# The sample state update of a gated linear recurrence mixer as two 32-row tiles of the array

## The chip, the core and the metric

One core of a Trainium2 chip runs the whole program. The metric is the device time of one execution in microseconds (us); the kernel before was timed three times.

## What is computed

The program is one inference step of a two-layer decoder: a recurrent mixer (HGRN2) and a convolutional feed-forward in layer 0, attention and feed-forward in layer 1, for a prompt of 512 tokens and for 8 sampled sequences of 8 tokens each. All of it is float32. The change lies in the mixer, in the state of the sampled sequences. For each of 8 heads (128 key and 128 value features) the reference does, cut to what matters:

```python
b = jnp.cumsum(lc, axis=2)                      # running log decay inside a chunk
o = (einsum('bhts,bhsv->bhtv', A, vc)           # inside the chunk
     + einsum('bhtd,bhdv->bhtv', qc * exp(b), S))
S = (exp(b_last)[..., None] * S                 # the old state, decayed
     + einsum('bhsd,bhsv->bhdv', kc * exp(b_last - b), vc))
o = rmsnorm(o, g_onorm) * silu(g)
```

For the sampled tokens there are 8 states of 128x128, one per sequence, and each sequence adds the product of its own 8 keys and 8 values. So with the 64 tokens of the samples side by side, token s may only reach the state of sequence s // 8.

## The kernel before

Five engines run programs written out by hand: SP issues the loads of weights, ACT and DVE work elementwise, POOL (GpSimd) too and issues some DMAs, PE multiplies. Semaphores order them; each engine takes its own work strictly in the order written. Tiles live in fixed places, PSUM is `acc` (four banks for the projections) and `aux` (four banks for all else, `aux[:, 0]` to `aux[:, 3]`).

The mixer is a pipeline over heads. `mixer(t, par, front, rec, tail)`, which every engine has, does in one block: `front`, the four projections of head t; `rec`, the recurrence of head t - 1 (masked products `gram` at seven levels, transposes of V and K, the prompt's state `ds`); `tail`, the end of head t - 2 (output products `outs`, the state update of the samples, the norm `onorm`). The blocks are mixer(1), a loop over mixer(2) to mixer(7), mixer(8) without projections, and mixer(9), which has only the tail. So mixer(2) to mixer(9) carry a tail each.

On PE a projection is `gemm` (L1353): for each of 8 slices of the inner dimension three pairs of products of 128x288 (the operands are split in a high and a low part), and the table `quarters` says after which slice of which of the four projections which step is put between. Where `front` is false the steps follow each other bare. After mixer(9) the output projection (L1353 too, `acc<-ol,w_hi`) begins at once, slice by slice as the heads' `ol` is there.

The sample state of a head goes through these places:

- ACT copies the transposed V and K of the 64 sample tokens to `Vs` and `kTs` (64 rows of 128). DVE has set rows 64 to 127 of `kTs` and of `Vb` to zero once at the start (L884, L885).
- POOL spreads `Vs` to `Vb` (L1216): for each of 8 sequences 128 columns, and by the mask `blk` all rows are zero but that sequence's 8. So `Vb` is 64 x 1024 on top of 64 rows of zeros.
- PE, `state(c)` (L1441), for c = 0, 1: all 128 rows of `kTs` times 512 columns of `Vb`, four sequences, both into the one bank `aux[:, 2]`. state(0) stands behind `outs` in the first quarter, state(1) at the start of the second, and it waits (`s1_ok`) until DVE has emptied the bank.
- POOL multiplies the old states by the decay into `S1` (L1208); DVE, `new_state(c)` (L769), adds the bank to four states of `S1` (the profile calls this tile mix_S). new_state(0) stands behind the products of level 0, new_state(1) behind the next w_lo, late in the block.
- `onorm` (L1446, L1447), in the first quarter four slices behind `outs`, writes the mean squares of the output to `aux[:, 3]`; ACT makes `orr` of them, DVE multiplies into `og` (L807 to L813), ACT and DVE split it in `oh` and `ol` (L823).

Other steps that the prediction names: `As` times `Vs` (L1436) is a product over 64 rows, the last of `outs`; `gram` products of the samples (L1388) have 64 columns of weights; z j is DVE's product of level j (L745, L746), difference j is L735, L736; w_lo is L707; h is updated at L909. In the decode attention of layer 1, L1597 issues per call four products with `tile_position=(0, 32 * g)`, each 32 columns of weights wide, for g = 0 to 3. Its neighbours L1565, L1602 and L1604 use the whole array.

```python
def state(c):
    pe.wait_ge(vb_ok, td + 1)
    wait(pe, s1_ok, 2 * td + c) if c else None
    nc.tensor.matmul(aux[:, 2, :], kTs[:], Vb[:, 4 * c:4 * c + 4, :], start=True, stop=True).then_inc(s1_ps, 1)
```

## Time and profile before

| what | us |
|---|---|
| median of 3 runs | 1780.14 (1779.13 to 1781.63) |
| the profiled execution, its own time | 1781.3 |
| its span, first to last instruction | 1779.7 |
| PE, matmul busy | 1709.6 |
| DVE busy | 940.2 |
| ACT busy | 658.2 |
| POOL busy | 307.3 |
| state products L1441, 32 passes, median of one | 0.592 |
| additions L769, 16, median of one | 0.678 |

A float32 product shows as two passes ("x2" for one product), with a load of weights (PEld) each. A pass is shown from its start to its modelled end, so neighbours overlap: what a product takes from the array is the distance between starts, not the length shown. "128*64" in a row is rows by columns of the weights, "128x288" the shape that is written or streamed. Passes of the projection have one pass per product, and a pair covers 576 columns. The granted clock over the whole run is 0.989 of 2.4 GHz.

### The profile page before, as it was taken

The numbers are of one execution on the slowest core, as the hardware profiler recorded it, in microseconds if no ns is written. First come the engines' busy times: TensorE is split into PE (matmuls) and PEld (weight loads), VectorE is DVE, ScalarE is ACT, GpSimd is POOL, SyncE is SP. The second block draws the span as 40 slices with busy tenths as digits, with TensorE's granted clock in tenths as the row PEclk, the third lists the DMA queues.
The fourth block names the chain that finished last, engine by engine and source line by source line (L and its number), as shares of the span: only waits on it lengthen the run. The fifth ranks groups of instructions, "written<-read, shape, count | busy, mean of one in ns | idle before, by whom it ended". The sixth has DMA issues, their size and how long they took to land.

```text
span 1779.7 us, 33926 instructions
## 1 busy us (share of the span) xinstructions
PE 1709.6 (96%) x12754; PEld 1619.7 (91%) x12754; DVE 940.2 (53%) x1593; ACT 658.2 (37%) x1057; POOL 307.3 (17%) x362
## 2 busy tenths in 40 slices
PE   5999999989999999999999998888899999999997
PEld 5999999969999999999999997555589999999997
DVE  5788888875455555332443434444455555554221
ACT  4544444533433333222333444333333333333111
POOL 3222222212222222000000001111012222221000
PEclk8999999989999999999999999999999999999999
DMA  4222222212222222222233352555613222222331
GB/s 173 62 81 76 72 72 74 70 51 84 87 83 82 82 82 80 82 87 86 91 116 119 97 174 73 184 186 190 197 48 87 84 82 82 82 82 82 106 92 39
DMA packets 79236, 171.76 MB, mean 97 GB/s; under 512 B 6738, under 2 KB 40802, under 8 KB 79170
## 3 DMA queue, kind: packets, MB, share of 16 engines
q1 hardware_dynamic: 73218, 149.84, 27.4%
q0 software_dynamic: 5952, 21.02, 3.4%
q8 instruction: 44, 0.72, 0.2%
q14 instruction: 22, 0.18, 0.0%
HBM read 158.56 MB, written 12.27 MB: 96 GB/s over the span
## 4 chain that ended last, share of the span: by engine, by line
PE 89%; DMA 3%; DVE 2%; issue 2%; ACT 1%; SPq 1%; POOL 0%; DVEq 0%; ACTq 0%; POOLq 0%
PE acc L1353 75%; PE aux L1380 3%; DMA dec_Kd<-cache_k_in 3%; PE acc L1565 2%; PE acc L1583 1%; PE aux L1597 1%; SPq L351 1%; PE aux L1513 1%; PE aux L1441 1%; PE aux L1434 1%; PE aux L1388 1%; DVE xl L713 1%; PE acc L1573 1%; PE aux L1393 1%; PE aux L1419 0%
## 5 line engine op out<-in xcount | busy, mean ns | idle before, releaser
L1353 PE MATMUL acc<-xl,w_hi 128*128 128x288 f32 x2192 | 488.0, 304 | 21.6 <-DVE w_lo L707 16.6
L1353 PE MATMUL acc<-xh,w_hi 128*128 128x288 f32 x2192 | 472.0, 297 | 0.0
L1353 PE MATMUL acc<-xh,w_lo 128*128 128x288 f32 x2192 | 471.6, 297 | 0.0
L707 DVE TENSOR_TENSOR w_lo<-w_raw,w_hi 128x1024 fp32r<-128x1024 f32 (+1 forms) x217 | 283.6, 1307 | 337.6 <-ACT w_hi L382 334.2
L1353 PEld LDWEIGHTS acc<-xl,w_hi 128*128 128x128 f32 x2192 | 355.2, 190 | 35.1 <-DVE w_lo L707 17.3
L1353 PEld LDWEIGHTS acc<-xh,w_lo 128*128 128x128 f32 x2192 | 355.8, 190 | 0.0
L1353 PEld LDWEIGHTS acc<-xh,w_hi 128*128 128x128 f32 x2192 | 355.7, 190 | 0.0
L382 ACT ACTIVATE w_hi<-w_raw 128x1024 fp32r<-128x1024 f32 (+1 forms) x217 | 224.2, 1033 | 240.3 <-PE acc L1353 206.0
L1353 PE MATMUL acc<-ffn_glo,w_hi 128*128 128x288 f32 x704 | 151.0, 295 | 0.0
L1353 PE MATMUL acc<-ffn_gh,w_lo 128*128 128x288 f32 x704 | 149.8, 293 | 0.0
L1353 PE MATMUL acc<-ffn_gh,w_hi 128*128 128x288 f32 x704 | 148.9, 293 | 0.0
L1353 PEld LDWEIGHTS acc<-ffn_gh,w_lo 128*128 128x128 f32 x704 | 112.8, 188 | 0.0
L1353 PEld LDWEIGHTS acc<-ffn_gh,w_hi 128*128 128x128 f32 x704 | 112.4, 187 | 0.0
L1353 PEld LDWEIGHTS acc<-ffn_glo,w_hi 128*128 128x128 f32 x704 | 111.9, 187 | 0.0
L1256 POOL TENSOR_TENSOR ffn_sil<-ffn_sil,rms 128x576 f32<-128x576 f32 x44 | 63.3, 1438 | 255.2 <-ACT ffn_sil L546 255.2
L542 ACT ACTIVATE ffn_a<-ffn_u,gains 128x512 f32<-128x512 f32 x88 | 50.5, 621 | 110.8 <-DVE ffn_u L937 110.7
L546 ACT ACTIVATE ffn_sil<-ffn_a 128x576 f32<-128x576 f32 x44 | 30.2, 686 | 142.3 <-DVE ffn_a L950 142.3
L1170 POOL TENSOR_TENSOR ssq<-ssq,sq 128x576 f32<-128x576 f32 x25 | 37.6, 1503 | 257.1 <-ACT sq L570 129.8
L652 ACT ACTIVATE att_Pr<-acc,att_nm 128x128 f32<-128x128 f32 (+1 forms) x64 | 33.7, 527 | 108.5 <-DVE att_nm L1072 78.8
L1072 DVE CUSTOM_DVE_ANT_0 acc<-acc,att_NC 128x128 f32<-128x128 f32 (+1 forms) x64 | 31.9, 498 | 76.2 <-PE acc L1566 75.7
L549 ACT ACTIVATE ffn_gh<-ffn_sil 128x576 f32 (+1 forms) x44 | 30.2, 686 | 107.2 <-DVE ffn_sil L958 107.2
L948 DVE SCALAR_TENSOR_TENSOR ffn_a<-ffn_u,gains,ffn_a 128x512 f32<-128x512 f32 x88 | 65.9, 748 | 6.0 <-DVE ffn_a L950 1.7
(250 smaller groups left out, 2449.6 us busy)
## 6 DMA issues: line engine op xcount, KB each, us to landing
w_raw<-w_fi_in SPq DMA_DIRECT2D x88, 512.0 KB, 3.6
w_raw<-w_mix_in SPq DMA_DIRECT2D x32, 512.0 KB, 3.6
w_raw<-w_fo_in SPq DMA_DIRECT2D x32, 512.0 KB, 3.5
dec_Kd<-cache_k_in SPq DMA_DIRECT2D x32, 512.0 KB, 6.9
dec_Vd<-cache_v_in SPq DMA_DIRECT2D x32, 512.0 KB, 5.9
w_raw<-w_kv_in SPq DMA_DIRECT2D x17, 512.0 KB, 3.7
w_raw<-w_o_in SPq DMA_DIRECT2D x16, 512.0 KB, 3.6
w_raw<-w_qg_in SPq DMA_DIRECT2D x16, 512.0 KB, 3.6
```

The source lines that it names most:

```text
L382: nc.scalar.activation(w_hi[:, pos.slot % SPL, 0:width], w_raw[:, pos.slot, 0:width], ACT.Copy)\
L542: nc.scalar.activation(dst, src, ACT.Identity, scale=col_of(gains, cw + 2 * FT + f), bias=col_of(gains, G_CB + FT * layer + f)).then_inc(c ...
L546: nc.scalar.activation(sil[:], a_[:], ACT.Silu).then_inc(sil_ok, 1)
L652: nc.scalar.activation(Pr[:, x % 2, 0:w], S_ps(x % 2)[:, 0:w], ACT.Exp, scale=-1.0, bias=nm[:, x:x + 1], accum_out=rs[:, x:x + 1]).then_in ...
L707: nc.vector.tensor_tensor(w_lo[:, pos.slot % SPL, 0:width], w_raw[:, pos.slot, 0:width], w_hi[:, pos.slot % SPL, 0:width].bitcast(F32), AL ...
L948: nc.vector.scalar_tensor_tensor(out=a_[:, 0:SEQ], in0=u[:, j:j + SEQ], scalar=w, in1=a_[:, 0:SEQ], op0=ALU.mult, op1=ALU.add)
L1072: nc.vector.tensor_tensor_reduce(out=s, in0=s, in1=NC[:, k, x // 4, 0:w], scale=-1.0, scalar=3.0e38, op0=ALU.add, op1=ALU.min, accum_out=n ...
L1170: nc.gpsimd.tensor_tensor(ssq[:], ssq[:], src[:], ALU.add).then_inc(ssq_done, 1)
L1256: nc.gpsimd.tensor_tensor(sil[:], sil[:], rms[:], ALU.mult).then_inc(silr_ok, 1)
L1353: mm = nc.tensor.matmul(acc[:, tp, hf, 0:HALF], W[:, sp_, 128 * j:128 * j + 128], X[:, kt, HALF * hf:HALF * hf + HALF], start=(first and j ...
L1380: mm = nc.tensor.matmul(aux[:, g % 2, CH * c:CH * c + CH], lhs[:, CH * c:CH * c + CH], rhs[:, CH * c:CH * c + CH], start=True, stop=True)
L1565: nc.tensor.matmul(s[:, 0:w], QX[:, k, a, P * tb:P * tb + P], tile_of(KT, i)[:, 0:w], start=True, stop=False)
```

## The change

The 64 sample tokens are cut in two groups of 32, four sequences each. Each group is a product over 32 rows of the array, placed by `tile_position` at rows 0 and 32, and each has its own bank, `aux[:, 2]` and `aux[:, 3]`. `Vb` holds in each group of rows only that group's four sequences, so it has 64 x 512 elements and no zero rows below; the mask constant is folded accordingly. Both products stand in the first quarter, behind `outs`; the step at the start of the second quarter is gone. DVE does both additions one after the other, before qd. Since `aux[:, 3]` was also used by `ds` before and is used by `onorm` after, `state` now waits for the last `s_step` and `onorm` for both `s1_ok`.

```diff
@@ -145,8 +145,8 @@
         eb = mx("eb", [P, T]); qd = mx("qd", [P, T]); kd = mx("kd", [P, T])
         E = mx("E", [P, 2, T]); Z = mx("Z", [P, 2, T])
         A = mx("A", [P, NCH, P]); As = mx("As", [NS, NS])
-        V = mx("V", [P, NCH, P]); Vs = mx("Vs", [NS, P]); Vb = mx("Vb", [P, NSEQ, P])
-        kT = mx("kT", [P, NCH, P]); kTs = mx("kTs", [P, P])
+        V = mx("V", [P, NCH, P]); Vs = mx("Vs", [NS, P]); Vb = mx("Vb", [NS, NSEQ // 2, P])
+        kT = mx("kT", [P, NCH, P]); kTs = mx("kTs", [NS, P])
         S = mx("S", [P, NCH, P])
         S0 = mx("S0", [P, NSEQ, P]); S1 = mx("S1", [P, NSEQ, P])
         orr = mx("orr", [P, T]); og = mx("og", [P, T])
@@ -467,7 +467,7 @@
                     rec_exp(hd, 3)
                     act.wait_ge(kT_ps, hd + 1)
                     nc.scalar.activation(kT[:], aux[:, 3, :].rearrange("p (c s) -> p c s", c=NCH), ACT.Copy).then_inc(kT_ok, 1)
-                    nc.scalar.activation(kTs[0:NS, :], aux[0:NS, 2, 0:P], ACT.Copy).then_inc(kT_ok, 1)
+                    nc.scalar.activation(kTs[:], aux[0:NS, 2, 0:P], ACT.Copy).then_inc(kT_ok, 1)
                 if front:
                     softlog(qr, ql, qr_ok, q_t, t, q_ok)
                 if rec:
@@ -763,10 +763,10 @@
 
                 def new_state(c):
 
-                    dve.wait_ge(s1_ps, 2 * td + c + 1)
+                    dve.wait_ge(s1_ps, td + 1)
                     dve.wait_ge(s0_mul, td + 1)
                     s1 = S1[:, 4 * c:4 * c + 4]
-                    nc.vector.tensor_tensor(s1, s1, aux[:, 2, :].rearrange("p (n v) -> p n v", n=4), ALU.add)\
+                    nc.vector.tensor_tensor(s1, s1, aux[:, 2 + c, :].rearrange("p (n v) -> p n v", n=4), ALU.add)\
                         .then_inc(s1_ok, 1)
 
                 if front and not (isinstance(t, int) and t == 0):
@@ -794,6 +794,7 @@
                     zed(hd, rp, 0)
                 if tail:
                     new_state(0)
+                    new_state(1)
                 if rec:
                     dve.wait_ge(eb_ok, hd + 1)
                     wait(dve, o_ps, hd)
@@ -818,7 +819,6 @@
                     nc.vector.sem_inc(evac, 1)
                     lo(Pos(2, t, 4))
                 if tail:
-                    new_state(1)
                     dve.wait_ge(oh_ok, td + 1)
                     nc.vector.tensor_tensor(tile_of(ol, td), og[:], tile_of(oh, td).bitcast(F32), ALU.subtract)\
                         .then_inc(ol_ok, 1)
@@ -881,8 +881,6 @@
             nc.vector.memset(eps[:], EPS).then_inc(setup, 1)
             nc.vector.memset(A[:], 0.0)
             nc.vector.memset(As[:], 0.0)
-            nc.vector.memset(kTs[NS:P, :], 0.0)
-            nc.vector.memset(Vb[NS:P], 0.0)
             dve.wait_ge(ld_gain, 16)
             for m in range(DT):
                 gain_lo(xl, xh, m, G_MIX, m)
@@ -1212,9 +1210,10 @@
                 if rec:
 
                     pool.wait_ge(v_ok, 2 * hd + 2)
-                    wait(pool, s1_ps, 2 * hd)
-                    nc.gpsimd.tensor_tensor(Vb[0:NS], Vs[:].unsqueeze(1).to_broadcast([NS, NSEQ, P]),
-                                            blk[0:NS, :].unsqueeze(2).to_broadcast([NS, NSEQ, P]), ALU.mult).then_inc(vb_ok, 1)
+                    wait(pool, s1_ps, hd)
+                    nc.gpsimd.tensor_tensor(Vb[:], Vs[:].unsqueeze(1).to_broadcast([NS, NSEQ // 2, P]),
+                                            blk[0:NS, 0:NSEQ // 2].unsqueeze(2).to_broadcast([NS, NSEQ // 2, P]), ALU.mult)\
+                        .then_inc(vb_ok, 1)
             pool.dma_start(S0[:].rearrange("p n v -> p (n v)"), d["s0"][0]).then_inc(s0_in, 16)
             pool.wait_ge(ld_const, 80)
             mixer(0, 0, True, False, False)
@@ -1435,20 +1434,24 @@
                                          start=(n == 0), stop=False)
                     nc.tensor.matmul(o, Vs[:], As[:], start=False, stop=True).then_inc(o_ps, 1)
 
-                def state(c):
+                def state():
                     pe.wait_ge(vb_ok, td + 1)
-                    wait(pe, s1_ok, 2 * td + c) if c else None
-                    nc.tensor.matmul(aux[:, 2, :], kTs[:], Vb[:, 4 * c:4 * c + 4, :], start=True, stop=True).then_inc(s1_ps, 1)
+                    pe.wait_ge(s_step, 4 * td + 4)
+                    for c in range(2):
+                        r = slice(32 * c, 32 * c + 32)
+                        mm = nc.tensor.matmul(aux[:, 2 + c, :], kTs[r, :], Vb[r], start=True, stop=True, tile_position=(32 * c, 0))
+                    mm.then_inc(s1_ps, 1)
 
                 def onorm():
                     pe.wait_ge(s_step, 4 * td + 4)
                     pe.wait_ge(osq_ok, 2 * td + 2)
+                    pe.wait_ge(s1_ok, 2 * td + 2)
                     nc.tensor.matmul(aux[:, 3, :], mean_head[:], osq[:, 0:SEQ], start=True, stop=True)
                     nc.tensor.matmul(aux[:, 1, 64:64 + NS], mean_head[:], osq[:, SEQ:T], start=True, stop=True).then_inc(on_ps, 1)
 
                 quarters = (
-                    {1: [(tail, outs), (tail, lambda: state(0))], 5: [(tail, onorm)]},
-                    {0: [(tail, lambda: state(1))], 3: [(rec, gram_0)], 6: [(rec, lambda: gram(hd, rp, 1))]},
+                    {1: [(tail, outs), (tail, state)], 5: [(tail, onorm)]},
+                    {3: [(rec, gram_0)], 6: [(rec, lambda: gram(hd, rp, 1))]},
                     {0: [(rec, turn_v)], 2: [(rec, lambda: gram(hd, rp, 2))], 5: [(rec, turn_k)],
                      7: [(rec, lambda: gram(hd, rp, 3))]},
                     {1: [(rec, lambda: gram(hd, rp, 4))], 3: [(rec, ds)], 4: [(rec, lambda: gram(hd, rp, 5))],
@@ -1702,7 +1705,7 @@
     c[0:16, C_REP:C_REP + P] = (i[:16, None] == i[None, :] % 16)
     c[:, C_OWN:C_OWN + 2] = (i[:, None] // 16 % 2 == i[None, :2])
     c[:, C_SEQ:C_SEQ + 8] = (i[:, None] // 16 == i[None, :8])
-    c[0:NS, C_BLK:C_BLK + 8] = (i[:NS, None] // 8 == i[None, :8])
+    c[0:NS, C_BLK:C_BLK + 8] = (i[:NS, None] // 8 % 4 == i[None, :8])
     t = np.arange(T)
     c[:, C_KEEP:C_KEEP + T] = np.where(t < SEQ, t % CH != 0, t % DSEQ != 0)
     c[:, C_KEEPC:C_KEEPC + T] = np.where(t < SEQ, t != 0, t % DSEQ != 0)
```

The place on PE is the tail within the first quarter of a block in the loop: outs, then the state, then the projection, onorm and the rest of the quarter. Before:

```order
L1431 MATMUL aux<-mix_qd,mix_S 128x128
L1434 MATMUL aux<-mix_qd,mix_S_79 128x8 x8
L1436 MATMUL aux<-mix_As,mix_Vs 128x64
L1441 MATMUL aux<-mix_Vb,mix_kTs 128x512
L1353 MATMUL acc<-xl,w_hi 128x288 x2
L1353 MATMUL acc<-xh,w_lo 128x288 x2
L1353 MATMUL acc<-xh,w_hi 128x288 x2
```

and at the start of the second quarter, between two slices of projections:

```order
L1353 MATMUL acc<-xh,w_hi 128x288 x2
L87 REGISTER_ALU
L1441 MATMUL aux<-mix_Vb,mix_kTs 128x512
L1353 MATMUL acc<-xl,w_hi 128x288 x2
L1353 MATMUL acc<-xh,w_lo 128x288 x2
```

Of the change:

```order
L1430 MATMUL aux<-mix_qd,mix_S 128x128
L1433 MATMUL aux<-mix_qd,mix_S_79 128x8 x8
L1435 MATMUL aux<-mix_As,mix_Vs 128x64
L1439 REGISTER_ALU
L1442 MATMUL aux<-mix_Vb,mix_kTs 128x512 x2
L1352 MATMUL acc<-xl,w_hi 128x288 x2
```

Both products are now behind the 64-row product of As (the program has one more wait there, so lines are shifted), and no product stands at the start of the second quarter.

On DVE the place is the stretch from the products of level 0 to ol, in a block of the loop. Before:

```order
L746 TENSOR_TENSOR mix_Z<-mix_k,mix_E 128x4x64
L766 ISA
L769 TENSOR_TENSOR mix_S_80<-mix_S_80,aux 128x512
L800 TENSOR_TENSOR mix_qd<-mix_q,mix_eb 128x576
L744 REGISTER_ALU
L745 TENSOR_TENSOR mix_Z<-mix_q,mix_E 128x8x32
```

and further down in the same block, on DVE too:

```order
L706 REGISTER_ALU
L707 TENSOR_TENSOR w_lo<-w_raw,w_hi 128x1024
L769 TENSOR_TENSOR mix_S_80<-mix_S_80,aux 128x512
L823 ISA
L823 TENSOR_TENSOR mix_ol<-mix_og,mix_oh 128x576
```

Of the change:

```order
L746 TENSOR_TENSOR mix_Z<-mix_k,mix_E 128x4x64
L769 TENSOR_TENSOR mix_S_80<-mix_S_80,aux 128x512 x2
L801 TENSOR_TENSOR mix_qd<-mix_q,mix_eb 128x576
L744 REGISTER_ALU
L745 TENSOR_TENSOR mix_Z<-mix_q,mix_E 128x8x32
```

The second addition has moved ahead of qd, level 1 and difference 2, and w_lo is followed by ol.

## Rows read from the trace of the kernel before

**Rows 1.** Page, part 1: busy time, share of the span, instructions by engine.
```profile
PE 1709.6 (96%) x12754; PEld 1619.7 (91%) x12754; DVE 940.2 (53%) x1593; ACT 658.2 (37%) x1057; POOL 307.3 (17%) x362
```

**Rows 2.** Windows: per engine busy us (instructions); then PE clock, DMA share, GB/s.
```profile
172.00:210.00 38.00, 38.00 (x280) 35.43 (x280) 32.70 (x59) 19.90 (x33) 8.63 (x6) 1.00 0.27 85
357.00:363.00 6.00, 4.75 (x14) 2.24 (x14) 4.92 (x12) 2.90 (x8) 0.23 (x1) 0.72 0.28 87
372.00:378.00 6.00, 5.64 (x25) 5.42 (x26) 5.55 (x14) 1.67 (x3) 0.02 (x1) 0.50 0.00 0
```

**Rows 3.** Waits, 100 to 324 us: total, times, longest.
```profile
PEld acc L1353 <- issue: 8.7, 42, 0.2
```

**Rows 4.** Timeline of one head: start, us, engine, line, operation, count.
```profile
183.02 1.13 PE L1441 MATMUL aux<-mix_Vb,mix_kTs 128*128 128x512 f32 x2
...
184.25 0.42 PE L1353 MATMUL acc<-xh,w_lo 128*128 128x288 f32 x2
...
190.63 1.02 PE L1441 MATMUL aux<-mix_Vb,mix_kTs 128*128 128x512 f32 x2
...
191.76 0.43 PE L1353 MATMUL acc<-xh,w_lo 128*128 128x288 f32 x2
```

**Rows 5.** Timeline of PE in the decode attention, 1134 to 1146 us.
```profile
1138.47 0.69 PE L1597 MATMUL aux<-dec_Kd,att_Qb 128*32 128x288 f32 x8
1139.10 0.91 PE L1565 MATMUL acc<-kv_KT,att_QX 128*128 128x384 f32 x2
...
1142.86 1.14 PE L1602 MATMUL aux<-rms,dec_neg_rep 128*128 128x288 f32 x4
1143.84 0.19 PE L1604 MATMUL aux<-dec_bfc 128*128 128x64 bf16 x1
```

**Rows 6.** Timeline of PE around a 128x64 product, 171 to 176 us.
```profile
171.80 0.28 PE L1380 MATMUL aux<-mix_Z 128*128 128x128 f32 x1
...
174.05 1.05 PE L1380 MATMUL aux<-mix_Z 128*128 128x128 f32 x8
...
175.03 0.43 PE L1388 MATMUL aux<-mix_Z 128*64 128x128 f32 x2
...
175.77 0.42 PE L1353 MATMUL acc<-xh,w_lo 128*128 128x288 f32 x2
```

**Rows 7.** Timeline of the same head: first add, onorm, wait for orr.
```profile
185.23 0.68 DVE L769 TENSOR_TENSOR mix_S<-mix_S,aux 128x512 f32<-128x512 f32 x1
...
187.17 1.02 PE L1446 MATMUL aux<-mix_og,mix_mean_head 128*128 128x512 f32 x2
...
190.04 0.75 DVE L807 SCALAR_TENSOR_TENSOR mix_og<-aux,gains,mix_orr 128x512 f32<-128x512 f32 x1 [2.12 <-ACT mix_orr L448]
```

**Rows 8.** Timeline of mixer(8), PE and DVE, 357 to 363 us.
```profile
357.32 1.86 PE L1446 MATMUL aux<-mix_og,mix_mean_head 128*128 128x512 f32 x2 [0.26 <-ACT mix_og L438]
357.44 0.68 DVE L769 TENSOR_TENSOR mix_S<-mix_S,aux 128x512 f32<-128x512 f32 x1
...
362.17 1.16 PE L1380 MATMUL aux<-mix_q,mix_k 128*128 128x128 f32 x8 [0.99 <-DVE mix_og L809]
```

**Rows 9.** Timeline of mixer(8), 369 to 373 us: Vb and z 3.
```profile
369.96 2.06 POOL L1216 TENSOR_TENSOR mix_Vb<-mix_Vs,mix_blk 64x1024 f32<-64x1024 f32 x1
370.19 2.11 DVE L746 TENSOR_TENSOR mix_Z<-mix_k,mix_E 128x256 f32<-128x256 f32 x1
```

**Rows 10.** Timeline of mixer(9) and the start of the output projection.
```profile
387.66 1.10 PE L1446 MATMUL aux<-mix_og,mix_mean_head 128*128 128x512 f32 x2
387.86 0.69 DVE L769 TENSOR_TENSOR mix_S<-mix_S,aux 128x512 f32<-128x512 f32 x1 [5.02 <-PE aux L1441]
...
389.94 0.42 PE L1353 MATMUL acc<-mix_oh,w_lo 128*128 128x288 f32 x2
...
394.04 1.23 DVE L707 TENSOR_TENSOR w_lo<-w_raw,w_hi 128x1024 fp32r<-128x1024 f32 x1 [0.19 <-ACT w_hi L382]
...
396.02 0.43 PE L1353 MATMUL acc<-mix_ol,w_hi 128*128 128x288 f32 x2
```

## The prediction

> **What bounds the kernel now.** I read the page's busy shares first: PE is busy 96% of the span, DVE 53%, POOL 17% [rows 1]. The mixer is the first fifth of the run, so I looked at one of its heads by windows: in 172 to 210 us PE is busy all 38.00 us at granted clock 1.00, and DVE 32.70 us [rows 2]. The list of waits of that part names no engine that PE waits for; what is left is marked "issue" [rows 3]. While the projections run between a head's steps, PE time is therefore the head's time: an array product taken away gives all its time back, work of DVE, ACT or POOL taken away gives nothing, and a new wait costs only where it ends after PE would have arrived. Six heads, those of mixer(2) to mixer(7), are like this. mixer(8) and mixer(9) have no projection in between, and there PE does wait: these two are costed apart. A difference of 0.2%, 3.6 us, is about what a measurement can tell from no change.
>
> **The state products now.** A float32 product appears as two passes, x2. The first, state(0), starts at 183.02; the second projection pair after it starts at 184.25, a pair takes 0.26 to 0.27 (23 of them lie between 389.94 and 396.02 [rows 10]), so state(0) held the array 1.23 - 0.27 = 0.96 us [rows 4]. state(1) starts at 190.63, the second pair after it at 191.76: 1.13 - 0.27 = 0.86 us, that is 0.43 per pass of 512 columns. The 0.1 us by which state(0) is dearer comes with the change of tile form ahead of it (the 64-row product of As). Together 1.82 us per head.
>
> **Do two tiles overlap?** No row tiles of this size are in the trace, but column tiles are: the decode scores issue four float32 products of 128x32, eight passes of 288 columns, and the next product starts 0.63 us after the first [rows 5]. Passes of 288 columns that can't overlap take 0.98 / 4 = 0.245 us each in the same rows (L1602), so eight in turn would be 1.96 us; two passes are 0.49. The four tiles ran side by side, with some 0.14 us for going in and out of the tile form. I take the same for two row tiles: both passes of both in the time of one product, 0.96 us with the change of form ahead of it, as now. By the Trainium skill, "TensorE: Matmul & The Clock Gate", section Part 3: Packing small matmuls, matmuls start and end strictly in program order; taken for whole products in two passes, this puts the second tile's first pass beside the first tile's second, three pass times where two would do, and by the rule the sum below would be +0.4 us instead of -2.7. These rows speak against it (five pass times, 1.2 us, where 0.63 stand), and the measurement decides; row tiles, which write all 128 partitions of two banks at once, no row here shows.
>
> **What the new form costs.** Leaving it for the 128-row projection is new. Nearest row: the 128x64 product at 175.03 sits between full forms [rows 6]. The eight passes before it, 0.28 each (171.80), overlap to 1.05 us, so they follow each other every 0.11; ten passes and a pair would take 1.10 + 0.27 = 1.37, they took 175.77 - 174.05 = 1.72. That is 0.35 for two changes of form, 0.17 for one. Bounds: 0 (the 64-row product is entered without a visible gap) and 0.35. I take 0.17. A head's products then cost 0.96 + 0.17 = 1.13 us instead of 1.82: **-0.69 us, times 6 = -4.1 us.**
>
> **The new waits in these six heads.** onorm now also waits for both adds of DVE. The first add starts at 185.23 [rows 7], after z 0, long after both tiles are done (183.02 + 1.1, 184.9 even in turn); at 0.68 each the second ends by 186.6. PE reaches onorm at 187.17, with the new form 0.2 later. Cost 0, margin 0.5 us or more. state's wait for the last s_step costs nothing, since outs just ahead of it waits for gram_used, which DVE signals after s_step. On DVE the second add moves from behind w_lo to ahead of qd: qd, z 1 and difference 2 come 0.7 later, into the 2.12 us in which DVE waits for orr [rows 7]. Queued behind onorm are only projections; ACT's Ln is asked for when onorm ends, as before. POOL's Vb has 64x512 instead of 64x1024, some 0.9 us less, also for DVE, which is held while POOL works; PE does not wait for either, so 0. turn_v's wait for s1_ok is met earlier. The memsets removed stand at the start, where DVE then waits for the gains and for ACT: 0.
>
> **mixer(8).** onorm started at 357.32, right after ACT's squares [rows 8]. Now it has to wait for two adds: the first can start at 357.44 as now, since with overlap both tiles are done when state(0) was; at 0.68 each the two end at 358.80, and onorm starts at 358.85: +1.5. Behind it queue gram 0, which needs og and so orr, then the turn of V: all shift by 1.5; state(1), now gone from there, filled time in which PE waited for og anyway (0.99 idle at 362.17). Then one thing is given back: DVE's z 3 product took 2.11 us and ended at 372.30, just after Vb on POOL did at 372.02 [rows 9]; products of its kind take a fraction where POOL rests. Vb at half size ends about 1.0 us sooner. **+0.5 us** net; bounds -0.2 and +1.5.
>
> **mixer(9).** Here DVE waited for state(0) (first add at 387.86, the end of its product) [rows 10]. The adds will end at 389.23, onorm start at 389.3 instead of 387.66, +1.6. The output projection started 0.27 before 389.94, at 389.67, which is 2.01 after onorm; 0.86 of that was state(1). Now 1.15 remain, and it starts at 390.4: +0.75. All its inputs are there but the last, ol, which the first seven of eight steps give time. The next weights' w_lo ended at 395.27 and shifts by 1.6 to 396.9; the second tile of the projection would start at 396.02 + 0.75 = 396.8. With the hand-over that is some 0.15 more. **+0.9 us**, bounds +0.7 and +1.6.
>
> **Sum.** -4.1 + 0.5 + 0.9 = -2.7 us against the profiled execution of 1781.3 us (span 1779.7). That run is 1.2 above the median 1780.14; the difference carries over, so 1780.1 - 2.7 = **1777.4 us**. With the bounds of the form change alone the sum goes from -3.7 to -1.6.
>
> **Rivals.**
> 1. The two tiles run one product after the other, because both write all partitions of PSUM, or because the array keeps them apart. Per head 0.86 more, six times +5.2; mixer(8) +0.5, mixer(9) +0.86: -2.7 + 6.5 = +3.8, **1783.9 us**, slower. It decides against the change from the point where the second tile ends over 0.36 us after the first (2.7 / 7.6: six heads in full, the other two in part), and reaches 0.2% only if nothing overlaps. For it: no row of two row tiles. Against: four column tiles read four streams at once [rows 5]. Chance 0.12.
> 2. Half overlap: the second tile's first pass waits for the first tile's second. 0.43 more per head: -2.7 + 2.6 + 0.1 + 0.4 = +0.4, **1780.5 us**. For it: in-order issue would do it. Against: rows 5. It is what the rule of the Trainium skill's page "TensorE: Matmul & The Clock Gate", named above, would give. Chance 0.12.
> 3. The clock. PE will idle some 1.8 us in mixer(8) and 1.5 us in mixer(9) ahead of onorm. In the trace the granted clock was 0.72 over 357 to 363 (PE had idled just before) and 0.50, the lower of the two levels, over 372 to 378, when PE had waited for the z 3 product of rows 9 [rows 2]. If the output projection starts at 1.2 GHz like one of these, it loses 0.28 x 6 = 1.7 to 0.50 x 6 = 3.0 us: -1.0 to +0.3, **1779.1 to 1780.4 us**. Chance 0.14.
> 4. Leaving the form costs nothing and mixer(8) gives Vb's time back in full: -3.7 to -4.4, **about 1776 us**. Chance 0.06.
>
> **How the numbers follow.** My forecast has 0.56. The range leaves out rival 1 (0.12) above and a little of the measurement's own spread below: 1775.2 to 1781.6. Faster by over 0.2% means below 1776.6: a third of the forecast's own spread (the form change between 0 and 0.17, the runs' own 1 us) and most of rival 4, 0.23. Slower by over 0.2%, above 1783.7: rival 1, of which nearly half falls just short, and a little for a wait I don't see, 0.09. The rest, 0.68, is within.
>
> **What would show it.** In the new profile, the state line has four passes per head; right is: two start within 0.05 us of each other, the other two 0.43 to 0.55 later, the projection goes on 1.1 to 1.2 us after the first, and a head is 0.7 us shorter. Two starts 0.43 apart three times, or a step of 1.9 us, is rival 1. No wait of PE before onorm in the six heads; in mixer(8) and mixer(9) onorm starts 0.05 to 0.1 after the second add. Vb near 1 us. If PE is shown waiting for DVE inside a projection, or a head does not get shorter, the prediction is wrong in its main term; if heads shorten by 0.7 and the total does not move, the two bare blocks or the clock took it.

## The result and the profile after

The changed kernel took 1788.55 us (median of 6 runs, 1787.63 to 1791.02), beside 1780.76 for the kernel before on the same chip (6 runs, 1777.90 to 1783.31). The ratio is 1.0047, 95% interval 1.0034 to 1.0060: slower by 0.47%, +7.8 us, where 1777.4 was forecast and 1781.6 was the upper end of the range. The profiled execution took 1790.42 us, span 1788.8; before it was span 1779.7. The rows below explain the 9.1 us between the two spans.

The page, part 1, of the changed kernel (busy us, share of the span, instructions):

```profile
PE 1714.8 (96%) x12754; PEld 1626.1 (91%) x12754; DVE 932.2 (52%) x1591; ACT 658.2 (37%) x1057; POOL 296.4 (17%) x362
```

Beside [rows 1], DVE and POOL do less, as meant, and PE is busy 5.2 us *longer*, although it was given less to do. So the time is not in waits alone; PE's own work became slower. The windows say where. Each row is one of the six heads of the loop of the changed kernel, from state product to state product; columns as in [rows 2]:

```profile
94.95:139.17 44.22, 44.22 (x323) 41.73 (x322) 36.84 (x67) 21.31 (x36) 10.94 (x8) 0.96 0.24 74
139.17:183.41 44.24, 44.24 (x324) 41.75 (x323) 36.84 (x67) 21.34 (x36) 10.94 (x8) 0.96 0.24 74
183.41:227.60 44.19, 44.19 (x323) 41.70 (x322) 36.81 (x67) 21.31 (x36) 10.94 (x8) 0.96 0.23 72
227.60:271.85 44.25, 44.25 (x323) 41.75 (x322) 36.82 (x67) 21.33 (x36) 10.93 (x8) 0.96 0.24 73
271.85:314.55 42.70, 42.70 (x324) 40.21 (x323) 36.83 (x67) 21.33 (x36) 10.95 (x8) 1.00 0.24 75
314.55:359.87 45.32, 44.27 (x312) 41.12 (x311) 36.14 (x66) 20.95 (x36) 10.95 (x8) 0.92 0.19 59
```

and two of the same heads in the kernel before:

```profile
183.02:226.36 43.34, 43.34 (x323) 40.65 (x322) 37.69 (x67) 21.32 (x36) 12.45 (x8) 1.00 0.24 74
313.04:355.93 42.89, 41.84 (x311) 39.08 (x311) 37.01 (x66) 20.96 (x36) 12.46 (x8) 1.00 0.20 63
```

One head, at 271.85, has granted clock 1.00 throughout. It is 42.70 us long, 0.64 less than 43.34: that is the forecast's main term (-0.69). The other five have a lower mean clock and are longer than before, four of them by 0.85 to 0.91, the last, where the low stretch is twice as long, by 2.43. A head without the fall being 42.70, the fall costs about 44.22 - 42.70 = 1.5 us. Cut finer, the third head of the changed kernel reads (windows of it):

```profile
183.40:185.20 1.80, 1.80 (x10) 1.04 (x10) 1.41 (x3) 1.80 (x5) 0.60 (x1) 1.00 0.01 2
185.20:188.70 3.50, 3.50 (x17) 3.50 (x16) 3.50 (x9) 1.23 (x4) 0.00 (x0) 0.51 0.49 150
188.70:192.00 3.30, 3.30 (x23) 2.82 (x22) 0.20 (x1) 1.49 (x3) 0.00 (x0) 1.00 0.00 0
```

The clock is at its lower level (0.50, 1.2 GHz) for 3.4 us right behind the state products, and PE is busy for every one of these microseconds: it did not idle before it fell. The timeline of PE in that head of the changed kernel (it begins inside the run of 16 passes of 128x8):

```profile
181.85 1.26 PE L1433 MATMUL aux<-mix_qd,mix_S 128*128 128x8 f32 x10
183.04 0.43 PE L1435 MATMUL aux<-mix_As,mix_Vs 64*128 64x64 f32 x2
183.41 1.13 PE L1442 MATMUL aux<-mix_Vb,mix_kTs 32*128 32x512 f32 x4
184.46 0.53 PE L1352 MATMUL acc<-xl,w_hi 128*128 128x288 f32 x2
184.83 0.42 PE L1352 MATMUL acc<-xh,w_lo 128*128 128x288 f32 x2
...
185.90 0.69 PE L1352 MATMUL acc<-xh,w_lo 128*128 128x288 f32 x2
...
189.25 1.02 PE L1449 MATMUL aux<-mix_og,mix_mean_head 128*128 128x512 f32 x2
```

The four passes of the two tiles take about the time of one product (their starts in the trace are 183.405, 183.412, 183.938 and 183.945); the projection resumes 1.06 us after the first, and its first pair takes 0.37 instead of 0.26. From 185.2 to 188.7 pairs take 0.48 instead of 0.26. Both adds (L769) are done by 186.9, and onorm starts at 189.25, without a wait.

The two bare blocks, timeline of PE and DVE of the changed kernel, mixer(8) first:

```profile
359.87 1.13 PE L1442 MATMUL aux<-mix_Vb,mix_kTs 32*128 32x512 f32 x4
...
361.37 1.28 DVE L769 TENSOR_TENSOR mix_S<-mix_S,aux 128x512 f32<-128x512 f32 x2
...
362.80 2.05 PE L1449 MATMUL aux<-mix_og,mix_mean_head 128*128 128x512 f32 x2 [1.80 <-DVE mix_S L769]
...
367.84 2.08 PE L1379 MATMUL aux<-mix_q,mix_k 128*128 128x128 f32 x8 [2.67 <-DVE mix_og L810]
...
375.63 1.21 POOL L1214 TENSOR_TENSOR mix_Vb<-mix_Vs,mix_blk 64x512 f32<-64x512 f32 x1
...
390.77 1.13 PE L1442 MATMUL aux<-mix_Vb,mix_kTs 32*128 32x512 f32 x4
...
391.94 1.28 DVE L769 TENSOR_TENSOR mix_S<-mix_S,aux 128x512 f32<-128x512 f32 x2 [5.04 <-PE aux L1442]
...
393.37 1.96 PE L1449 MATMUL aux<-mix_og,mix_mean_head 128*128 128x512 f32 x2 [1.48 <-DVE mix_S L769]
...
395.41 0.83 PE L1352 MATMUL acc<-mix_ol,w_hi 128*128 128x288 f32 x2
```

Against [rows 8] and [rows 10]: the waits before onorm are there as forecast, 1.80 and 1.48 us. In mixer(9) onorm and the start of the output projection then run at the lower clock (window of the changed kernel):

```profile
393.46:396.87 3.41, 3.41 (x10) 2.38 (x11) 0.00 (x0) 1.15 (x3) 0.54 (x1) 0.50 0.38 154
```

**Where the time went.** From the first loop head's state product to mixer(8)'s the kernel before takes 355.93 - 96.34 = 259.59 us and the changed one 359.87 - 94.95 = 264.92: +5.33. From there to the first record of the output projection (389.27 before, 395.41 now) 33.34 became 35.54: +2.20. That stretch in the kernel before and, below it, in the changed one:

```profile
355.93:389.27 33.34, 25.94 (x139) 19.36 (x139) 24.99 (x49) 10.21 (x22) 7.63 (x7) 0.85 0.10 36
```

```profile
359.87:395.41 35.54, 24.94 (x139) 19.24 (x139) 24.49 (x50) 9.93 (x21) 7.31 (x8) 0.83 0.11 40
```

PE is idle 10.60 us of it instead of 7.40, which is the two new waits, and busy 1.00 us less. Of the +2.20, mixer(8) has only 0.13 (from state product to state product 30.77 before, 30.90 now) and mixer(9) 2.07 (2.57 before, 4.64 now). Ahead of the first loop head the profiled execution was 1.39 us quicker; it spent 3.4 us less at the lower clock there, and so did e1 below, whose rows are full. Together +6.1. The next 714.0 us, FFN, kv and prompt attention, add 0.3. The remaining 2.7 are in the decode attention; first its window in the kernel before, then in the changed kernel:

```profile
1103.25:1282.21 178.96, 157.35 (x1284) 102.36 (x1285) 76.92 (x309) 68.39 (x213) 19.83 (x54) 0.99 0.60 191
```

```profile
1109.72:1291.36 181.64, 159.29 (x1284) 103.68 (x1285) 77.03 (x309) 68.32 (x213) 19.79 (x54) 0.97 0.59 188
```

There PE waits for transfers in both kernels, its clock is lower in the changed one, and no instruction of this stretch differs. The changed kernel's profile has one more stretch at the lower clock in it, 6.8 us from 1164.9. The profiles of e1, e2, e6 and e7 below have such an extra stretch too, those of e3, e4, e5, e8 and e10 do not, so it follows neither the tiles nor the falls in the heads. From the first decode product to the end the kernel before takes 675.9 us, the changed one 678.6, e1 679.0, e4 675.5. Why is not settled.

### The profile page after: what moved, and what is told of

It is laid out like the page before. It is cut to its first block, busy times and chain, and to the rows that moved or that the text cites. A ratio compares the mean times of both kernels' runs of the same rounds, so it can differ in the third digit from the quotient of the medians.

```text
span 1788.8 us, 33915 instructions
## 1 busy us (share of the span) xinstructions
PE 1714.8 (96%) x12754; PEld 1626.1 (91%) x12754; DVE 932.2 (52%) x1591; ACT 658.2 (37%) x1057; POOL 296.4 (17%) x362
## 4 chain that ended last, share of the span: by engine, by line
PE 89%; DMA 3%; DVE 3%; issue 2%; ACT 1%; SPq 1%; POOL 0%; DVEq 0%; ACTq 0%; POOLq 0%
PE acc L1352 76%; DMA dec_Kd<-cache_k_in 3%; PE aux L1379 3%; PE acc L1568 2%; PE acc L1586 1%; PE aux L1600 1%; SPq L351 1%; PE aux L1516 1%; PE aux L1433 1%; DVE xl L713 1%; PE aux L1387 1%; PE aux L1392 1%; PE acc L1576 1%; PE aux L1449 1%; PE aux L1442 0%
```

## The experiments

The clock could fall because the products no longer occupy all 128 rows (the full-row theory); because of the 32-row tile form itself; or because of the new order and waits. These differ in whether tiles are needed, and in whether a clock fall follows the tiles or something ahead of them. The short runs of products ahead of the state (eight pairs of 128x8, then the 64-row As product, 2.1 us in all) are a fourth candidate, which e3 and e4 brought forward. The expectations use letters: A is that little work in the array (few rows, short products) lets the clock fall, B the new order and waits, C the 32-row form, D that a full float32 product is missing behind the short run, E that any small change of this place does it, F that a long run of short products does it and the full product beside it was what held the clock.

In the tables "falls" are stretches at 0.50 in the six heads of the one profiled run; "head" is a head without one; "clock" is the range of the mean granted clock over the whole execution, for all runs of the median. A head of the kernel before is 43.34 with no fall in six, and its clock, in 78 executions beside the experiments, was 0.985 to 0.993; that of the change, in 6, was 0.980 to 0.982. In the code, `...` stands for lines left out.

### First four: rows, order, place

**e1_full_rows.** The change's order, waits and two banks, with full padded rows:

```diff
...
-                        mm = nc.tensor.matmul(aux[:, 2 + c, :], kTs[r, :], Vb[r], start=True, stop=True, tile_position=(32 * c, 0))
+                        mm = nc.tensor.matmul(aux[:, 2 + c, :], kTs[:], Vb[:, 4 * c:4 * c + 4, :], start=True, stop=True)
...
```

> The order, waits and banks of the change, but both state products over 128 padded rows as before (Vb 64x1024 again). Theory A, the tile form after the short sample products lets the granted clock fall: clock stays up in the six heads, a head 43.3 us as before, only the two bare blocks lose some 3 us, about 1784 us. Rival B, the new order and the longer waits before onorm do it: granted clock falls after the state products as in the change, heads of 44.2 us, about 1790 us.

**e2_rows64.** The kernel before, its two products over the 64 rows that hold data:

```diff
-        V = mx("V", [P, NCH, P]); Vs = mx("Vs", [NS, P]); Vb = mx("Vb", [P, NSEQ, P])
-        kT = mx("kT", [P, NCH, P]); kTs = mx("kTs", [P, P])
+        V = mx("V", [P, NCH, P]); Vs = mx("Vs", [NS, P]); Vb = mx("Vb", [NS, NSEQ, P])
+        kT = mx("kT", [P, NCH, P]); kTs = mx("kTs", [NS, P])
...
```

> The kernel before with its two products at their old places, but over 64 rows, without the rows of zeros. Theory A in the form that the rows of the array in use count: half the array is used as in the change, so the clock falls in some of the six heads, up to 1.7 us for each, 1783 to 1790 us. Rival A2, that only the time the array spends in short products counts, or the 32-row form itself: no fall, heads 43.3 to 43.5 us, 1780 to 1782 us.

**e3_samples_first.** The change with the short sample products and As ahead of the prompt's dense ones:

```diff
-                    for c in range(NCH):
...
                     for n in range(NSEQ):
...
-                    nc.tensor.matmul(o, Vs[:], As[:], start=False, stop=True).then_inc(o_ps, 1)
+                    nc.tensor.matmul(o, Vs[:], As[:], start=False, stop=True)
+                    for c in range(NCH):
...
+                    mm.then_inc(o_ps, 1)
```

> The change, but in outs the short products of the samples come first and the dense products of the prompt after them, so that 1.6 us of dense products stand between the short ones and the two tiles. Theory A, a long stretch of little work in the array lets the clock fall: no fall in the six heads, a head 42.7 us, about 1778 us. Rival C, the 32-row form alone does it wherever it stands: falls as in the change, about 1788.5 us.

**e4_tiles_q2.** The change with the tiles at the start of the second quarter, where state(1) used to be, in blocks with projections; there the adds come behind the next w_lo, and onorm does not wait for them:

```diff
...
-                    {1: [(tail, outs), (tail, state)], 5: [(tail, onorm)]},
-                    {3: [(rec, gram_0)], 6: [(rec, lambda: gram(hd, rp, 1))]},
+                    {1: [(tail, outs), (tail and not front, state)], 5: [(tail, onorm)]},
+                    {0: [(tail and front, state)], 3: [(rec, gram_0)], 6: [(rec, lambda: gram(hd, rp, 1))]},
```

> The change, but in blocks with projections the two tiles stand at the start of the second quarter, between dense projections (both additions behind w_lo); bare blocks as in the change. Theory A: no fall, a head 42.7 us, about 1778 to 1779 us. Rival C, the 32-row form alone: the clock falls after the tiles, about 1788 us.

| | median (runs) | ratio to before | falls | head | clock |
|---|---|---|---|---|---|
| e1_full_rows | 1782.60 (10) | 1.0010, 0.9998 to 1.0023 | 0 | 43.35 | 0.987 to 0.991 |
| e2_rows64 | 1789.78 (5) | 1.0054, 1.0035 to 1.0073 | 2 | 43.80 | 0.980 to 0.986 |
| e3_samples_first | 1794.43 (4) | 1.0081, 1.0062 to 1.0100 | 2, one twice as long | | 0.976 to 0.983 |
| e4_tiles_q2 | 1787.93 (5) | 1.0045, 1.0029 to 1.0060 | 4 | | 0.978 to 0.983 |

e1 and e2 came out as theory A had it. e3 and e4 missed: 1778 was forecast for both.

e1's timeline shows the two products in turn, and its window over the heads has the full clock:

```profile
181.07 1.98 PE L1443 MATMUL aux<-mix_Vb,mix_kTs 128*128 128x512 f32 x4
```

```profile
50.00:330.00 280.00, 280.00 (x2088) 263.85 (x2087) 242.32 (x423) 138.49 (x226) 74.63 (x50) 1.00 0.23 73
```

So the change's order and waits, taken alone, do nothing to the clock in the heads; what is left of them, 1.4 us (interval from none to 4), is about the bare blocks' two waits. The rows of zeros are what differs between e1 and the change.

e2 has no tile and no new wait, only half the rows, and loses clock too (its profiled run, 1796.35 us, is the slowest of its five). Its windows, a head without and one with a fall:

```profile
96.36:140.16 43.80, 43.80 (x323) 40.45 (x322) 37.37 (x67) 21.42 (x36) 11.39 (x8) 1.00 0.24 74
183.57:228.86 45.29, 45.29 (x324) 41.68 (x324) 37.36 (x67) 21.43 (x36) 11.38 (x8) 0.96 0.22 71
```

Even at full clock its head is 0.46 longer than 43.34: two products in the 64-row form cost more than padding. Most of it, 0.37, is at state(1), which alone goes from the 128-row form into the narrow one and back.

In e3 and e4 the fall comes *before* the tiles. e3's timeline, where the dense 128-row products behind As already take 0.21 a pass instead of 0.11, and then e4's:

```profile
93.52 0.43 PE L1430 MATMUL aux<-mix_As,mix_Vs 64*128 64x64 f32 x2
...
95.22 0.64 PE L1433 MATMUL aux<-mix_A,mix_V 128*128 128x128 f32 x2
...
97.07 1.28 PE L1443 MATMUL aux<-mix_Vb,mix_kTs 32*128 32x512 f32 x4
```

```profile
181.59 0.43 PE L1438 MATMUL aux<-mix_As,mix_Vs 64*128 64x64 f32 x2
...
183.98 0.68 PE L1355 MATMUL acc<-xl,w_hi 128*128 128x288 f32 x2
...
190.31 1.13 PE L1447 MATMUL aux<-mix_Vb,mix_kTs 32*128 32x512 f32 x4
```

In e4 the tiles come at 190.31, 7 us after the clock fell and 4 us after it had risen; none of its falls follows them. The 32-row form as the cause was now in doubt. What the kernels that lost clock have in common, and e1 and the kernel before do not, is that no full-row state product stands right behind the short run.

### Next three: attempts to mend it

**e5_split_outs.** e4 with the prompt's dense products split around the short run. 

> Tiles at the start of the second quarter as in e4, and the short products of the samples set between two halves of the prompt's full float32 products instead of behind them, so that full float32 products stand on both sides as in the kernel before. Theory D, the clock falls where the short products and As are not followed by a full float32 product: no fall in the six heads, a head 42.7 us, mixer(8) and mixer(9) as in the change; about 1779 to 1781 us. Rival C or E (any small change of this place, or the tiles themselves, lets it fall): 1787 us or more.

```diff
...
+                    prompt(0)
+                    prompt(1)
                     o = aux[:, 1, 0:NS]
                     for n in range(NSEQ):
...
+                    nc.tensor.matmul(o, Vs[:], As[:], start=False, stop=True)
+                    prompt(2)
+                    prompt(3).then_inc(o_ps, 1)
...
```

**e6_extra_full.** The change plus one full 128x512 product of constants ahead of the tiles; nobody reads it.

```diff
+                    nc.tensor.matmul(aux[:, 2, :], mean_head[:], keep[:, 0:SEQ], start=True, stop=True)
                     for c in range(2):
```

> The change, with one more full product of constants (128 rows, 512 columns, its result overwritten) between As and the two tiles. Theory D: it costs 0.86 us per head but the clock stays up, a head 43.5 to 43.6 us, about 1783 to 1784 us, less than the change although it does more. Rival C, the 32-row form itself lets the clock fall: falls as in the change, and 0.86 us per head more, about 1795 us.

**e7_late_state.** e5 with the bare blocks' tiles behind onorm, mixer(9)'s between two slices of the output projection, so that onorm waits for no add. Lines against e4 and the change:

```diff
...
-                    {1: [(tail, outs), (tail and not front, state)], 5: [(tail, onorm)]},
-                    {0: [(tail and front, state)], 3: [(rec, gram_0)], 6: [(rec, lambda: gram(hd, rp, 1))]},
+                    {1: [(tail, outs)], 5: [(tail, onorm)]},
+                    {0: [(tail and rec, state)], 3: [(rec, gram_0)], 6: [(rec, lambda: gram(hd, rp, 1))]},
...
+                         mid={3: last_state} if m == 0 and b_in == B_FI0 else None)
...
```

> e5, and in mixer(8) and mixer(9) too the tiles come behind onorm (after orr), in mixer(9) between slices of the output projection, so that onorm waits for no addition. Theory D: no fall in the six heads; mixer(8) and mixer(9) lose their 2.4 us or more of waiting before onorm; about 1776 to 1778 us, less than both kernels. If the clock falls in the bare blocks as often as in the change, up to 3 us more.

| | median (runs) | ratio to before | falls | clock |
|---|---|---|---|---|
| e5_split_outs | 1792.42 (5) | 1.0062, 1.0045 to 1.0080 | 2 | 0.978 to 0.982 |
| e6_extra_full | 1797.12 (4) | 1.0082, 1.0062 to 1.0102 | 1, twice as long | 0.982 to 0.984 |
| e7_late_state | 1790.21 (7) | 1.0040, 1.0025 to 1.0056 | 5 | 0.979 to 0.984 |

All three missed. Dense 128-row products behind the short run do not replace the state product. In e5 and e7 the falls begin 0.3 to 0.6 us after the start of As, when these products have hardly begun; both kernels also took half of them from ahead of the run, so this is no clean test of what stands behind it. A full product of constants helps in part: one fall instead of five, at a cost of 1.07 us per head (43.77 without a fall, 42.70 in the change). From the first head to mixer(8) it takes 265.3 us beside the change's 264.9, it loses more in the bare blocks, and it is the slowest of all. Its timeline shows that fall starting even so:

```profile
271.13 1.12 PE L1440 MATMUL aux<-mix_keep,mix_mean_head 128*128 128x512 f32 x2
272.18 2.02 PE L1443 MATMUL aux<-mix_Vb,mix_kTs 32*128 32x512 f32 x4
```

### Three that separate tiles from the short run

**e10_state_apart.** The kernel before, its full-row state(0) moved two slices later. No tile, no padding removed, no work added or taken away:

```diff
-                    {1: [(tail, outs), (tail, lambda: state(0))], 5: [(tail, onorm)]},
+                    {1: [(tail, outs)], 3: [(tail, lambda: state(0))], 5: [(tail, onorm)]},
```

> The kernel before, full rows and all, with only state(0) moved two slices of the projection away from the short products; no tile of 32 rows anywhere. Theory F: the same work and the same order on every other engine, but the clock falls in 2 or more of the six heads, some 1784 to 1788 us. Rival C, only the 32-row form lets the clock fall: no fall, 1780 to 1782 us.

**e11_no_short.** The change without the eight 128x8 products (the sample tokens' output lacks its part from the carried state); the tiles stay.

```diff
-                    for n in range(NSEQ):
-                        nc.tensor.matmul(o[:, DSEQ * n:DSEQ * n + DSEQ], S0[:, n], qd[:, SEQ + DSEQ * n:SEQ + DSEQ * (n + 1)],
-                                         start=(n == 0), stop=False)
-                    nc.tensor.matmul(o, Vs[:], As[:], start=False, stop=True).then_inc(o_ps, 1)
+                    nc.tensor.matmul(o, Vs[:], As[:], start=True, stop=True).then_inc(o_ps, 1)
```

> The change without the eight short products of the samples (their part of the output is left out), the tiles where the change has them. Theory F: no fall in the six heads, each 0.64 us for the tiles and 1.78 us for the short products shorter than before, 40.9 us; about 1764 to 1767 us. Rival C: falls behind the tiles in most heads, 1772 us or more.

**e8_spread.** The change with the eight short products two by two behind four slices of the projection, tiles in the second quarter, onorm two slices later. In the bare blocks there are no slices, and the eight still stand in one piece.

```diff
...
-                    {1: [(tail, outs), (tail, state)], 5: [(tail, onorm)]},
-                    {3: [(rec, gram_0)], 6: [(rec, lambda: gram(hd, rp, 1))]},
+                    {1: [(tail, outs)], 2: [(tail, lambda: samples(1))], 3: [(tail, lambda: samples(2))],
+                     4: [(tail, lambda: samples(3)), (tail and not front, state)], 7: [(tail, onorm)]},
+                    {2: [(tail and front, state)], 3: [(rec, gram_0)], 6: [(rec, lambda: gram(hd, rp, 1))]},
```

> Tiles in the second quarter (after its third slice), the eight short products spread two by two behind four slices of the projection, onorm two slices later. Theory F, the granted clock falls where many short products stand together and a full float32 product beside them was what just held it: no fall in the six heads, each 0.69 us shorter than before; mixer(8) and mixer(9) lose 2 to 4 us as in the change; about 1778 to 1781 us. Rival C, the 32-row tiles themselves pull the clock down: falls behind the tiles, 1787 us or more.

| | median (runs) | ratio to before | falls | head | clock |
|---|---|---|---|---|---|
| e10_state_apart | 1786.98 (10) | 1.0034, 1.0022 to 1.0045 | 2 | 43.33 | 0.983 to 0.989 |
| e11_no_short | 1775.80 (10) | 0.9969, 0.9954 to 0.9983 | 0 | 42.07 | 0.985 to 0.990 |
| e8_spread | 1783.00 (12) | 1.0010, 0.9998 to 1.0022 | 0 | 42.88 | 0.982 to 0.986 |

e10 is the cleanest of the study. Windows of it: a head with a fall, and the fall, whose 3.5 us have PE busy throughout:

```profile
222.77:267.73 44.96, 44.96 (x325) 41.72 (x324) 37.77 (x67) 21.31 (x36) 12.46 (x8) 0.96 0.23 71
```

```profile
226.00:229.50 3.50, 3.50 (x12) 2.47 (x12) 1.70 (x4) 1.94 (x5) 0.35 (x1) 0.51 0.48 150
```

Only the place of one product changed, and two heads of 43.34 became some 44.95. The fall begins at 226.04, before the moved product starts at 227.05. The two profiled falls explain 3.2 us; over its ten runs the kernel loses 6.2. The profiled run was one of its fastest (1783.38 us, clock 0.987), so others probably had more falls. Both the time and the falls are what its expectation gave for F.

e11 has the tiles in every head and not one fall. Its timeline and a head's window:

```profile
177.60 0.43 PE L1432 MATMUL aux<-mix_As,mix_Vs 64*128 64x64 f32 x2
177.97 1.13 PE L1439 MATMUL aux<-mix_Vb,mix_kTs 32*128 32x512 f32 x4
```

```profile
135.90:177.97 42.07, 41.25 (x308) 38.45 (x307) 36.83 (x67) 21.33 (x36) 10.80 (x8) 1.00 0.25 78
```

PE is idle for 0.82 us of that head (42.07, busy 41.25). The waits of two heads of e11 name it:

```profile
PE aux L1446 <- DVE mix_S L769: 1.6, 2, 0.8
```

With the short products gone PE reaches onorm before DVE has added. The wait that the change put there, free in the change itself, costs 0.8 a head as soon as PE gains more than the margin, and that is most of what is missing to the 40.9 expected. In total e11 missed its 1764 to 1767: the six heads give 7.7 us, but the bare blocks take 1.2 more than before, with 10.2 us at the lower clock. There the clock fell without any short run, after PE had been idle for 3.0 of 3.4 us.

e8 has everything that the change has, short products too, and no fall either:

```profile
97.20:140.08 42.88, 42.88 (x324) 40.22 (x323) 36.89 (x67) 21.37 (x36) 10.94 (x8) 1.00 0.24 76
```

Its head keeps 0.46 of the 0.64 us, and yet the kernel is not faster: six times 0.46 is 2.8, and the bare blocks and the first products behind them spend it. The 1778 to 1781 forecast was missed, the heads without a fall were not. Over 330 to 400 us their clock is 0.85, where the kernel before has 0.93; e8's row first, then that of the kernel before:

```profile
330.00:400.00 70.00, 59.09 (x383) 52.04 (x382) 50.70 (x99) 25.86 (x45) 12.60 (x11) 0.85 0.16 54
```

```profile
330.00:400.00 70.00, 61.55 (x412) 53.40 (x410) 54.66 (x103) 27.56 (x48) 16.07 (x14) 0.93 0.17 56
```

### Two that look for a better version

Both are e8 with full products of constants in the two bare blocks: **e12_spread_fill** has two of them behind the tiles, **e13_fill_before** one before and one behind. The lines are those of e13.

```diff
...
+                def filler():
+                    pe.wait_ge(evac, 31)
+                    nc.tensor.matmul(acc[:, 0, 0, :], mean_head[:], keep[:, 0:SEQ], start=True, stop=True)
...
+                    if not front:
+                        filler()
                     for c in range(2):
...
```

> e8, and in mixer(8) and mixer(9) two full float32 products of constants behind the tiles, into a free bank, in the time in which the array waits for the additions. Theory F: the fall behind the bare tiles at 354 us (10.2 us at the lower level in e8) goes or gets shorter, the six heads stay as in e8; 1777 to 1781 us, below e8 by 2 us or more. If the fall stays, e8 plus up to 0.3 us, about 1783 us.

> e12 with one of the two full products between As and the tiles instead of behind them, which puts 0.86 us on the path of each bare block. Theory F: falls in the bare blocks go or get shorter too; 1778 to 1782 us. If neither e12 nor this shortens them, what stands beside the short products is not what decides in the bare blocks.

e12: 1783.76 us (12 runs), ratio 1.0011, 1.0001 to 1.0021; the bare blocks' clock stayed at 0.85, the case its expectation puts at about 1783. e13: 1779.37 us (12 runs, 1775.13 to 1791.85), ratio 1.0004, 0.9986 to 1.0021. In its profiled run the bare blocks lost only two stretches of 3.4 us:

```profile
330.00:400.00 70.00, 61.47 (x404) 52.36 (x403) 51.88 (x99) 25.97 (x45) 12.62 (x11) 0.95 0.16 55
```

Its span was 1778.4, 1.3 under the kernel before. But over twelve runs time goes with the mean clock, from 1775.13 us at 0.993 to 1791.85 at 0.980, and no gain can be told from none. No version of the whole computation beat the kernel before.

## Why the prediction was wrong

- **Do the tiles overlap:** right. Four passes in the time of two, as the column tiles of [rows 5] suggested. The Trainium skill's rule that matmuls start and end strictly in program order ("TensorE: Matmul & The Clock Gate", Part 3: Packing small matmuls) holds here pass by pass: first passes of both tiles 0.007 us apart, then the second passes. Taken for whole products, as rival 2 did, it does not. (The records do not name the tile of a pass; that the pairs 0.007 us apart are one pass of each tile is read from their starts.)
- **The price of the form:** right in size. From the first pass to the projection's first pass 1.06 us, plus 0.11 in its longer first pair, against 1.13 forecast; the head at full clock is 0.64 shorter instead of 0.69. "TensorEngine Tiling (Array Packing)", Key Properties, of the Trainium skill says that a change of tiling mode drains the engine; the traces agree in so far as a change costs some 0.1 to 0.2 us (0.11 here on leaving, 0.37 for in and out at e2's state(1)). They do not show a drain as such.
- **No new wait in six heads:** right; onorm comes after the adds in every one. Vb took 1.21 us in mixer(8) beside 2.06 [rows 9]; "near 1 us" was forecast.
- **mixer(8), mixer(9):** the waits were right (1.80 and 1.48 us of idle PE). The output projection came 2.20 us later against mixer(8)'s state product; +0.5 + 0.75 was forecast. mixer(8) cost 0.13, less than its 0.5; mixer(9) cost 2.07, above its upper bound of 1.6. Some 0.9 of that is in one place: from the start of onorm to the projection 2.04 us pass (393.37 to 395.41), where onorm up to state(1) took 1.10 before (387.66 to 388.76), the same two products. That is the lower clock, from 393.46 to 396.87; rival 3 was real, if a little ahead of the place it named and smaller than its 1.7 to 3.0.
- **The step that failed** is the sentence "an array product taken away gives all its time back", and with it the sum's six times -0.69. It was true only at constant clock. Rival 3 saw the clock as a danger after idle time in the bare blocks, and read its own row so: 0.72 over 357 to 363, "PE had idled just before". It hardly had. In the kernel before, timeline and windows of mixer(8):

```profile
353.79 1.85 PE L1434 MATMUL aux<-mix_qd,mix_S 128*128 128x8 f32 x16
```

```profile
354.10:357.50 3.40, 3.14 (x19) 2.25 (x19) 3.01 (x8) 3.37 (x8) 0.60 (x1) 1.00 0.00 0
357.50:360.90 3.40, 3.40 (x6) 1.20 (x5) 2.63 (x7) 2.10 (x5) 0.00 (x0) 0.50 0.50 154
```

PE was busy 3.14 of the 3.40 us ahead of that fall, much of it with the short run. The sign that the clock can fall behind the short run without much idle time was there before the change; in the loop I read granted clock 1.00 [rows 2] as a given, because PE was busy 100%. It was not a given. PE can be busy all the time and still fall to 1.2 GHz. Four heads lost 0.85 to 0.91 net, the last one 2.4, one gained 0.64: +5.3 where -4.1 stood. With +2.2 from the bare blocks that is the mixer's part of the result.

**What holds and loses the clock.** Behind the short run stands, in the kernel before, a full-row float32 product of 512 columns, half of it rows of zeros. With it there, no head in the profiled runs of two kernels (before, e1) had a fall, and the clock over all their executions lies in the same range. In the bare mixer(8) it is not enough: there the kernel before falls at 357.5, with the same product right behind the run and 0.26 us of idle time. Taking it from there brought falls as long as the short run stood in one piece: narrower rows (the change, e2), the tiles elsewhere (e3, e4, e5, e7), the same full-row product merely moved (e10), and, fewer, with a product of constants in its place (e6). The tiles alone do not: without the short run (e11) or with it spread out (e8, e12, e13) the heads with projections have no fall. So in these heads the cause is the pair: a run of short products, and little full-row work right behind it. Shown are both halves: e1 against the change and e10 against the kernel before for the full-row product, e11 against the change and e8 for the short run. In the bare blocks idle time comes in too, and the two are not separated there. Why the prompt's dense products do not do the same service as the state product (e5) stays open. So do the 2.7 us of the decode attention.

Why some heads of one run are hit and others not is not shown either, but the traces give a hint. In the changed kernel the falls begin 1.55, 1.70, 1.84 and 2.02 us behind the first tile in the first four heads, then one head has none, then 0.40 behind it. The first four are 44.37 us apart each time, as neighbouring falls are in e4, e5, e7 and e10, and a head with a fall is about as long. So a head that is hit puts the next one nearly in the same place, and where a head's steps lie in time seems to count beside what they are. The rows speak against a mere shift in time as the whole cause: the six heads of the kernel before, 43.34 apart, drift by 1 us each against that step, and none is hit. No run varied the time alone. The counts of falls come from one profiled run per kernel, and heads of one run are not independent; the mean clock of all executions leans the same way, though it counts the bare blocks too (e8: no fall in the heads, clock 0.982 to 0.986).

## What to carry to other kernels

On an engine that is never idle, work removed is only worth its time if the clock stays up; padding rows of zeros beside a run of short products may be what keeps it up. Before shrinking such a product, read the granted clock stretch by stretch on both sides of it; after the change, take the windows that hold the edit first, since busy shares look unchanged. Where short products can be spread between dense ones, do that first, and narrow the others then.

## What was not expected of the hardware

- The granted clock fell from 1.00 to 0.50 for 3.4 us with PE busy 100% on both sides, at about 1.5 us a time.
- Moving one full-row product by two slices (1.7 us of other work) cost 0.34% (e10).
- A product over 64 rows is not cheaper than one over 128 padded rows inside a 128-row stretch: a head was 0.46 us longer at full clock (e2).
- Two row tiles of 32 rows and 512 float32 columns, each writing a bank of all 128 partitions, run side by side with starts 0.007 us apart.
